# Weight slabs, rounded slabs and pages at several distances from a multiple of 128 bytes

## The reference

```python
def hybrid_layer(x, mem_n, ...):
    h = layer_norm(ALPHA * x + 0.5 * swiglu(x, ffn1_w_gu, ffn1_w_down), ...)
    (dn_q, dn_k, dn_v, dn_b, dn_a, dn_z, sw_q, sw_k, sw_v, xa_q, gates) = split(h @ w_in)
    o_dn = deltanet_branch(...)            # chunked gated delta rule, 4 heads
    o_sw = sliding_window_attention(...)   # 8 heads, window 128
    o_xa = memory_cross_attention(...)     # 4 heads, 256 memory rows
    merged = sum(sigmoid(gates) * einsum('bsnc,ncd->bsnd', branches, w_branch), axis=2)
    h = layer_norm(ALPHA * h + merged @ w_out, ...)
    return layer_norm(ALPHA * h + 0.5 * swiglu(h, ffn2_w_gu, ffn2_w_down), ...)

def reference(x, mem, ...):
    for l in range(2):
        x = hybrid_layer(x, layer_norm(mem), ...)
    x = x + token_mixer(rmsnorm(x), ...)   # four kinds of attention, gates, w_out
    x = x + conv_ffn(rmsnorm(x), ...)      # w_up, causal convolution over 3, gelu, w_down
    return rmsnorm(x)
```

## Time and profile before

| | us |
|---|---|
| median of the runs | 3521.11 (3520.66 to 3523.89) |
| profiled execution, its own time | 3520.0 |
| its span in the trace | 3518.2 |
| TensorE busy | 3457.2 |
| VectorE busy | 2226.0 |
| ScalarE busy | 1681.5 |
| mean granted clock of TensorE | 0.996 |

### The profile page before, as it was taken

One profiled execution on the slowest core, in us unless ns is written; L12 is line 12 of the kernel. 1 busy time (PEld: TensorE's weight loads), 2 busy tenths in 40 slices (PEclk: granted clock), 3 DMA queues, 4 the chain that ended last, 5 costly groups with the idle time before them and its releaser, 6 DMA issues.

```text
span 3518.2 us, 49763 instructions
## 1 busy us (share of the span) xinstructions
PE 3457.2 (98%) x19256; PEld 2940.1 (84%) x19256; DVE 2226.0 (63%) x4229; ACT 1681.5 (48%) x3243; POOL 111.5 (3%) x132
## 2 busy tenths in 40 slices
PE   9999999999999999999999999999999999999999
PEld 7998888877889998999888877888977677788887
DVE  5566666556775667566665566774666787666643
ACT  5355455554354545444555543553546443444432
POOL 0010000000000100010000000000100000000000
PEclk9999999999999999999999999999999999999999
DMA  5475331112335743474221112255622222233332
GB/s 156 133 173 145 119 96 46 49 46 67 96 101 139 171 126 99 135 174 129 90 70 45 52 58 87 87 147 138 160 89 89 61 70 86 75 95 97 96 97 89
DMA packets 198276, 358.86 MB, mean 102 GB/s; under 512 B 22102, under 2 KB 26359, under 8 KB 198040
## 3 DMA queue, kind: packets, MB, share of 16 engines
q1 hardware_dynamic: 178840, 321.32, 30.1%
q0 software_dynamic: 18432, 33.56, 5.7%
q10 hardware_dynamic: 768, 0.79, 0.1%
HBM read 350.60 MB, written 4.72 MB: 101 GB/s over the span
## 4 chain that ended last, share of the span: by engine, by line
PE 91%; DVE 5%; ACT 3%; issue 1%; DMA 0%; DVEq 0%; SPq 0%; ACTq 0%
PE bank L2492 21%; PE bank L2501 21%; PE bank L2493 20%; PE bank L2527 6%; PE bank L2530 6%; PE bank L2529 6%; PE bank L2480 2%; PE bank L2475 1%; PE bank L2570 1%; PE bank L2663 1%; DVE w_lo L3237 1%; PE bank L2673 1%; PE bank L2538 1%; DVE page_r L3279 1%; PE bank L2590 1%
## 5 line engine op out<-in xcount | busy, mean ns | idle before, releaser
L2492 PE MATMUL bank<-page_r,w_hi 128*128 128x512 f32 (+1 forms) x3446 | 1367.9, 397 | 25.4 <-DVE w_lo L3237 17.9
L2501 PE MATMUL bank<-page_r,w_lo 128*128 128x512 f32 (+1 forms) x3446 | 1343.4, 390 | 0.0
L2493 PE MATMUL bank<-page_r,w_hi 128*128 128x512 f32 (+1 forms) x3446 | 1332.1, 387 | 0.0
L2492 PEld LDWEIGHTS bank<-page_r,w_hi 128*128 128x128 f32 x3446 | 650.2, 189 | 170.1 <-DVE w_lo L3237 22.9
L2815 ACT ACTIVATE w_hi<-raw 128x512 fp32r<-128x512 f32 x864 | 532.5, 626 | 532.0 <-PE bank L2501 523.2
L2501 PEld LDWEIGHTS bank<-page_r,w_lo 128*128 128x128 f32 x3446 | 649.3, 188 | 129.5
L2493 PEld LDWEIGHTS bank<-page_r,w_hi 128*128 128x128 f32 x3446 | 650.5, 189 | 125.2 <-issue 3.6
L3237 DVE TENSOR_TENSOR w_lo<-raw,w_hi 128x512 fp32r<-128x512 f32 x864 | 574.4, 686 | 143.8 <-ACT w_hi L2815 141.7
L2527 PE MATMUL bank<-page_r,w_hi 128*128 128x256 f32 x1792 | 507.3, 283 | 2.4 <-DVE w_lo L3255 2.4
L2529 PE MATMUL bank<-page_r,w_hi 128*128 128x256 f32 x1792 | 507.1, 283 | 0.0
L2530 PE MATMUL bank<-page_r,w_lo 128*128 128x256 f32 x1792 | 507.1, 283 | 0.0
(11 more groups left out here) (322 smaller groups left out, 3457.2 us busy)
## 6 DMA issues: line engine op xcount, KB each, us to landing
raw<-weights SPq DMA_DIRECT2D x864, 256.0 KB, 2.6
raw<-pairs SPq DMA_DIRECT2D x320, 256.0 KB, 3.3
raw<-pairs POOLq DMA_DIRECT2D x128, 256.0 KB, 5.8
page_f<-x_t SPq DMA_DIRECT2D x8, 256.0 KB, 5.0
bias_rows<-page_f SPq DMA_DIRECT2D x8, 256.0 KB, 2.0
page_f<-bias_rows SPq DMA_DIRECT2D x8, 256.0 KB, 3.8
out_t<-page_f SPq DMA_DIRECT2D x12, 128.0 KB, 1.8
cst<-consts SPq DMA_DIRECT2D x4, 272.0 KB, 3.6
```

The costliest lines, as they stand in the source:

```text
L2492: self.e.matmul(o, hi, X.hi[kt], start=first, stop=False)
L2493: self.e.matmul(o, hi, X.lo[kt], start=False, stop=False)
L2501: last = self.e.matmul(o, lo, X.hi[kt], start=False, stop=final)
```

## The change

The starts of units and pages are moved by some bytes each. raw and w_hi get 64 more columns (256 bytes), and placed() works out where each unit starts: two neighbouring units share a distance from a multiple of 32 columns (128 bytes). For the seven pairs of raw units it is 0, 4, 8, 16, 24, 2 and 12 columns, that is 0, 16, 32, 64, 96, 8 and 48 bytes. For the nine w_hi units it is 0, 32, 64, 16 and 96 bytes (the last unit is alone). Between pages 17 and 18, 35 and 36, and 53 and 54 there are 32 bytes of padding, so that pages 0 to 17 start at 0 bytes, 18 to 35 at 32, 36 to 53 at 64 and 54 to 70 at 96 past a multiple of 128. The scratch tensor small shrinks from 2048 to 1184 columns to make room. first_line takes the place of line_end. A unit's slices count from its start in columns; a pair of units stays contiguous. cst stays at a multiple of 128 bytes; mean_rounded and gains stay at 96 bytes past one.

```diff
-LINE_END = 8
+SMALL = 1184
+SPARE = 64
+FIRST_LINE = 8
+SHIFTED = (18, 36, 54)
+RAW_PHASES = (0, 4, 8, 16, 24, 2, 12)
+HI_PHASES = (0, 8, 16, 4, 24)
+
+def placed(size, phases):
+    at, starts = 0, []
+    for phase in phases:
+        at += (phase - at) % 32
+        starts.append(at)
+        at += size
+    return starts
...
-        super().__init__(region[:, at * UNIT:(at + 1) * UNIT], rounded[:, at * UNIT:(at + 1) * UNIT])
+        super().__init__(region[:, at:at + UNIT], rounded[:, at:at + UNIT])
...
-        return self.region[:, self.at * UNIT:(self.at + 2) * UNIT]
+        return self.region[:, self.at:self.at + 2 * UNIT]
...
-        with nc.sbuf_tensor("w_lo", [P, NRAW * UNIT], F32R) as lo:
+        with nc.sbuf_tensor("w_lo", [P, NRAW * UNIT + SPARE], F32R) as lo:
...
-        self.small = sb("small", [P, 2048])
+        self.small = sb("small", [P, SMALL])
...
-        self.line_end = sb("line_end", [P, LINE_END])
+        sb("first_line", [P, FIRST_LINE])
         self.page_aps = []
         for i in range(PAGES):
+            if i in SHIFTED:
+                sb(f"line_part{i}", [P, 8])
...
+        raw_at = placed(UNIT, [RAW_PHASES[i // 2] for i in range(NRAW)])
+        hi_at = placed(UNIT, [HI_PHASES[i // 2] for i in range(NHI)])
+        self.raws = Units([Unit(memory.raw, memory.w_lo, raw_at[i], memory.s_raw[i], memory.s_added[i]) for i in range(NRAW)],
+                          LENT["raw"])
+        self.his = Units([Unit(memory.w_lent, memory.w_hi, hi_at[i], None) for i in range(NHI)], LENT["hi"])
```

More of the change, by code:

```diff
@@ L161, in wide @@
     def wide(self):
-        return self.region[:, self.at * UNIT:(self.at + 2) * UNIT]
+        return self.region[:, self.at:self.at + 2 * UNIT]
     def wide_rounded(self):
-        return self.rounded[:, self.at * UNIT:(self.at + 2) * UNIT]
+        return self.rounded[:, self.at:self.at + 2 * UNIT]
 class Stock:
@@ L443, in __init__ @@
         self.table, self.buckets, self.out = table, buckets, out
-        with nc.sbuf_tensor("w_lo", [P, NRAW * UNIT], F32R) as lo:
+        with nc.sbuf_tensor("w_lo", [P, NRAW * UNIT + SPARE], F32R) as lo:
             self.w_lo = lo
-        self.raw = sb("raw", [P, NRAW * UNIT])
-        with nc.sbuf_tensor("w_lent", [P, NHI * UNIT], F32) as lent:
+        self.raw = sb("raw", [P, NRAW * UNIT + SPARE])
+        with nc.sbuf_tensor("w_lent", [P, NHI * UNIT + SPARE], F32) as lent:
             self.w_lent = lent
-        self.w_hi = sb("w_hi", [P, NHI * UNIT], F32R)
+        self.w_hi = sb("w_hi", [P, NHI * UNIT + SPARE], F32R)
         self.cst = sb("cst", [P, NCONST])
@@ L519, in __init__ @@
         self.banks = Stock([Slot(b) for b in memory.bank_aps])
-        self.raws = Units([Unit(memory.raw, memory.w_lo, i, memory.s_raw[i], memory.s_added[i]) for i in range(NRAW)], LENT["raw"])
-        self.his = Units([Unit(memory.w_lent, memory.w_hi, i, None) for i in range(NHI)], LENT["hi"])
+        raw_at = placed(UNIT, [RAW_PHASES[i // 2] for i in range(NRAW)])
[3 more added lines that the diff above has]
+        self.his = Units([Unit(memory.w_lent, memory.w_hi, hi_at[i], None) for i in range(NHI)], LENT["hi"])
         self.pages = Stock([Slot(f, r) for f, r in memory.page_aps], self.raws, self.his)
@@ L536, in small @@
         self.small_at += n
-        assert a + n <= 2048
+        assert a + n <= SMALL
         return self.m.small[:, a:a + n]
```

## The result

| | before | after |
|---|---|---|
| median of the runs, us | 3521.11 (3520.66 to 3523.89) | 3549.35 (3545.96 to 3550.90) |
| profiled execution, us | 3520.0 | 3545.96 |
| its span, us | 3518.2 | 3544.2 |

The ratio is 1.0076, with a 95% interval from 1.0053 to 1.0099: the change makes the kernel 28 us slower, where I had forecast 193 and a range that began at 69. It lies between two of my cases, no cost (3521) and the low end of the range (3590), where I had put nothing.

What follows compares the result with a forecast made beforehand. TensorE was taken as the bound, by start-to-start product steps times their number. Displaced weight loads, 162 + 31 = 193 us, on the profiled 3520.0 gave 3713, so a median of 3714 us; range 3590 to 3910.

Steps and rivals of the forecast that it cites:

- slab loads: Slab transfers landing 8 to 96 bytes past a line: cost 0, hidden even at twice the landing time.
- element operations: ScalarE and VectorE work on moved operands: at most some 60 ns an operation, 0 on the path.
- smaller scratch: Scratch cut from 2048 to 1184 columns: said only to shift addresses, no cost counted.
- moving operands: Displaced moving operands of 13,337 large fp32r products: 0 taken, from L2499; up to 173 us kept for the range.
- weights, fp32r: Displaced weight loads of rounded products on TensorE: 12,454 at 13 ns each, 162 us.
- L2544's 13 ns: Extra time at L2544, weights 96 bytes past a multiple of 128, taken as the cost of one displaced weight load.
- Weights, fp32: Displaced weight loads of plain fp32 passes, where the load sets the pace: 2402 at 13 ns, 31 us.
- Six executions in two unlike neighbourhoods, all alike: L2544's executions in the trace before, cited as evidence that its weights' displacement costs time.
- rival 3: No cost: starts that count are shorter than 128 bytes, L2544 slow for its own reasons; 3521 us, chance 0.11.
- The faster rival: Large fp32r products starting weights and moving operand at different distances lose 13.3 ns: 171 us less, 3350; chance 0.03.
- 420 products in a 100 us window: Sign in the profile after: some 420 products of 512 columns in place of 442.
- 0.133 for 256 columns: Sign in the profile after: 256-column steps of 0.133 us in place of 0.120.

Runs made afterwards that it cites:

- mean_aligned: Kernel before with line_end allotted ahead of mean_rounded, moving mean_rounded from 96 to 128 past a multiple of 256; 3524.2 us beside 3522.0, one execution each.
- before_pages_down_128: Kernel before with scratch tensor small cut from 2048 to 2016 columns, so pages start 128 bytes lower; 3558.6 us, ratio 1.0107.
- all_at_32_again: Changed kernel with every raw slab, rounded slab and page at 32 bytes past a multiple of 128, run a second time; 3558.4 us, ratio 1.0102.
- all_at_64: Changed kernel with every raw slab, rounded slab and page at 64 bytes past a multiple of 128; 3557.1 us, ratio 1.0098.
- pages_moved: Changed kernel with all raw and rounded slabs at 0 bytes, pages still at 0, 32, 64 and 96; 3550.9 us, ratio 1.0085.
- weights_moved: Changed kernel with all pages at 0 bytes, raw and rounded slabs still at their mixed distances; 3550.9 us, ratio 1.0086.
- slabs_16_above: Changed kernel with all pages at 128 past a multiple of 256 and all slabs 16 bytes further on; 3543.4 us, one execution.
- weights_at_64: Changed kernel with all slabs, raw and rounded, at 64 bytes and all pages at 0; 3513.8 us over eight executions, ratio 0.9978.

## Why the prediction was wrong

The reading of what bounds the kernel held. TensorE's steps set the time, and the change came through them. What I expected to stay did: slab landings (2.8 us in the median, with 2.7 in the earlier trace rows), ScalarE's and VectorE's slab operations (627 and 685 ns), and TensorE's longest wait (15.5 us in total, with 17.9 in the earlier trace rows):

```profile
L2837 ACT ACTIVATE w_hi<-raw x864: 612/627/702, 4.2 to 3521.3; 128x512 fp32r<-128x512 f32 x173
...
DMA to landing us min/median/max: 2.4/2.8/7.6
```

```profile
PE bank L2514 <- DVE w_lo L3259: 15.5, 11, 5.7
```

The slab loads and the element operations, which I had set at nothing, cost nothing. The smaller scratch and the moving operands, which I had set at nothing too, did not: see below.

- **The step that failed first** is "weights, fp32r: 12,454 x 13 = 162 us". L2544's 13 ns are real, and mean_aligned shows that they come from its weights' place. But I took them for the price of a load off a multiple of 128, payable each time. They are what it costs to step once out of a settled row at distance 0 and back in. Where distances wander all the time, a step of 512 columns in a long row costs 5.4 ns more on average (232.1 against 226.7), whatever its own operands, and one of 256 columns 1.7 less. Summed, short rows included, the 9,080 steps of 512 columns give 44 us more and the 5,741 of 256 columns 9 less.
- **The line itself** was wrong: I counted around 128 bytes and from a fixed origin. before_pages_down_128 keeps all at multiples of 128 and is slower by more than the change; all_at_32_again and all_at_64 show that only the distance between slab and page counts. The change moved the pages by 128 around 256 as well, through the shorter scratch, which I had costed as "only shifts addresses"; before_pages_down_128 shows that such a shift alone can cost 37 us.
- **Weights, fp32, 31 us**: none. The steps between fp32 passes sum to 405.9 us before and 403.7 after, with 2402 of the 3252 displaced. That the load sets the pace there was no reason for it to pay.
- **Moving operands, 0 with 173 kept**: weights and pages aren't priced apart, so a sum with a term for each could not come out. pages_moved alone costs 30 us, weights_moved alone 30, and both together 28.
- **"Six executions in two unlike neighbourhoods, all alike"**, held against rival 3, were five in one neighbourhood; the sixth has uneven steps wherever its weights lie.
- **The rule of the Trainium skill**, third rival: "SBUF — State Buffer", in the part on the DMA port swizzle, has full bandwidth for accesses in one 16-byte cacheline, and I took from it that moves by whole lines are free. slabs_16_above moves all slabs by exactly 16 bytes and the 512-column step goes from 226.7 to 231.3 ns in the mean, so the runs disagree with that reading for TensorE's steps.
- **The faster rival** named the right quantity, the distance between the two operands, and drew the wrong sign from it for 512 columns. I dropped it because L2544, at a distance, was slower. For 256 columns it was right, and I had no row that could show it: no 256-column product of the kernel before is at a distance. I never asked whether the two widths could go opposite ways, so the low end of the range, 3590, held no case in which the 256-column products gain while the others lose.
- Of the signs to look for, 420 products in a 100 us window was forecast and 433 measured; 0.133 for 256 columns was forecast and 0.118 measured; the same steps whatever page they stream, as forecast.

## What to carry to other kernels

One odd operand in a settled pipeline prices a step out of and back into the pattern, not the pattern that a thousand odd ones make. Before multiplying such a price, ask which two addresses it could be a distance between, and around what; and vary that alone in a kernel where nothing else moves. For back-to-back float32r products it paid here to choose the distance between weights and moving operand and to try several, for each width by itself: 0 for 512 columns, 64 and 192 bytes for 256, together 36 us of 3521. A fixed distance is no gain by itself: 96 bytes in every product (3571 us) is slower than the mixture of the changed kernel (3549).

## What the runs showed of the hardware

- TensorE's step from one float32r product to the next depends on the distance between the start of the weights and that of the moving operand, counted around 256 bytes: 226.7 to 234.2 ns with 512 columns, 113.3 to 120.0 with 256, at a granted clock of 1.00. Neither place by itself was seen to matter (three kernels with distance 128 and their slabs at 128, 160 and 192 past a multiple of 256 have the same row of seven steps; distance 0 has 226.7 ns with both at 128 and with both at 192). fp32 passes don't show it: their steps sum to 403.7 us in the changed kernel, where most have their operands apart, and to 405.9 before. The Trainium skill, "TensorE: Matmul & The Clock Gate", in "Step-by-step: what each phase is for", gives the moving operand and the weight load independent read ports; in these runs the place of the weights against that of the moving operand changes the step by up to 7.5 ns (234.2 against 226.7), so for these products the two are not independent in time.
- Steps settle into rows that repeat. In the last feed-forward stage they are one step long at distance 0, three at 160 (231, 238, 231 ns), four at 224 and seven at 128. In column times of 2.4 GHz (0.417 ns), the sums of the one long and the three long come to 544 and 1680; 288, 272 and 560 also occur as means (120.0, 113.3, 233.3 ns). All are multiples of 16. What in the chip makes the pattern is open.
- Two different rows can be stable at one distance (117.8 and 113.3 ns with 256 columns at 64 and at 192; 226.7 and 233.3 with 512 columns at 16). weights_at_64's executions spread from 3508.8 to 3521.9 us, more than the 4 or 5 us of the kernel before beside it. A different pick among rows from one execution to the next would explain that; only one of its executions was traced, so it is not shown. Nor is it settled where its nearly 8 us come from (3513.8 against 3521.6 beside it): in its profile the 512-column steps cost 16 us more than before and the 256-column ones 17 us less, which leaves 1.
